# Moving one weight load up in SyncE's program order, at the boundary from the gate blocks to the first output projection

## The reference

```python
z = einsum("btd,dc->btc", rms_norm(x, mix_pre_g), w_in)
u, v, b_gate, c_gate, x_in, r_a, r_b = split(z)
u = gelu(u); v = layer_norm(gelu(v), ...)
y_a = einsum("btc,cd->btd", u * chunk_spatial_mix(v, w_s, b_s), w_a_out)
y_b = einsum("btc,cd->btd", b_gate * short_conv(c_gate * x_in, conv_w), w_b_out)
h = sigmoid(r_a) * y_a + sigmoid(r_b) * y_b
x = x + rms_norm(einsum("btd,de->bte", h, w_o), mix_post_g)
x = x + rms_norm(swiglu(rms_norm(x, ffn_pre_g), w_gate, w_up, w_down), ffn_post_g)
```

## Time and profile before

| what | value |
|---|---|
| time, median of 3 runs | 1629.03 us (1628.82 to 1631.62) |
| time of the profiled execution | 1628.98 us |
| span of the profiled execution | 1627.2 us |
| PE busy | 1608.6 us, 99% of the span |
| DVE / ACT / POOL busy | 64% / 33% / 42% of the span |
| DMA moved | 175.93 MB, mean 108 GB/s |
| mean granted clock of PE | 0.995 of full |

### The profile page before, as it was taken

How to read it: one execution, slowest core, us unless ns; L and a number is a source line. 1 busy time by engine, 2 the same in 40 slices (tenths; PEclk the granted TensorE clock), 3 DMA queues, 4 the chain that set the end, 5 groups by cost and what they waited for, 6 DMA issues and landing times.

```text
span 1627.2 us, 30359 instructions
## 1 busy us (share of the span) xinstructions
PE 1608.6 (99%) x12502; PEld 1554.3 (96%) x12502; DVE 1048.1 (64%) x1588; ACT 541.1 (33%) x816; POOL 679.6 (42%) x486
## 2 busy tenths in 40 slices
PE   8999999999999999899999999999999999999998
PEld 5889999999999999899978899999999999999998
DVE  7867867587583336865438875766666666575766
ACT  4222322222223335332232543222222233452544
POOL 1012444444444443642430216544444443455475
PEclk9999999999999999999999999999999999999999
DMA  5202011321313334353323412533333345572723
GB/s 211 80 0 79 27 53 34 98 79 34 98 60 106 106 106 140 111 177 105 103 100 106 141 47 78 156 105 105 105 105 105 106 126 166 185 234 79 235 104 132
DMA packets 145742, 175.93 MB, mean 108 GB/s; under 512 B 6909, under 2 KB 129397, under 8 KB 145605
## 3 DMA queue, kind: packets, MB, share of 16 engines
q1 hardware_dynamic: 145444, 173.96, 33.2%
q10 hardware_dynamic: 160, 0.04, 0.0%
HBM read 129.52 MB, written 44.49 MB: 107 GB/s over the span
## 4 chain that ended last, share of the span: by engine, by line
PE 93%; DVE 4%; DMA 1%; issue 1%; ACT 1%; POOL 0%; SPq 0%; DVEq 0%; POOLq 0%
PE ps L397 90%; PE ps L471 1%; DMA stage<-in_w_a_out 1%; DMA gv<-in_w_in 0%; DVE tp_f L1946 0%; PE ps L407 0%; PE ps L607 0%; DVE wv_lo_t L1608 0%; DVE small L1594 0%; DVE small L1593 0%; DVE small L1595 0%; DVE tp L1953 0%; PE ps L689 0%; DVE res L2086 0%; DVE q L2083 0%
## 5 line engine op out<-in xcount | busy, mean ns | idle before, releaser
L397 PE MATMUL ps<-tp,ring_hi 128*128 128x258 f32 x7340 | 1192.4, 284 | 6.6 <-POOL ring_lo L1012 6.3
L397 PEld LDWEIGHTS ps<-tp,ring_hi 128*128 128x128 f32 x7340 | 1018.9, 190 | 7.1 <-issue 6.8
L397 PE MATMUL ps<-tp,ring_lo 128*128 128x258 f32 x3670 | 750.4, 283 | 0.0
L397 PEld LDWEIGHTS ps<-tp,ring_lo 128*128 128x128 f32 x3670 | 575.9, 191 | 0.0
L1012 POOL TENSOR_TENSOR ring_lo<-stage,ring_hi 128x512 fp32r<-128x512 f32 (+1 forms) x202 | 311.2, 1550 | 452.2 <-ACT ring_hi L1147 451.9
L1012 POOL TENSOR_TENSOR ring_lo<-ring_f,ring_hi 128x512 fp32r<-128x512 f32 (+1 forms) x216 | 304.6, 1431 | 341.1 <-DVE ring_f L1702 195.7
L1147 ACT ACTIVATE ring_hi<-ring_f 128x512 fp32r<-128x512 f32 (+1 forms) x216 | 135.1, 627 | 481.0 <-DVE ring_f L1697 187.2
L1147 ACT ACTIVATE ring_hi<-stage 128x512 fp32r<-128x512 f32 (+1 forms) x202 | 123.2, 617 | 153.0 <-PE ps L397 85.4
L1694 DVE TENSOR_TENSOR ring_f<-stage 128x512 f32<-128x512 f32 (+1 forms) x54 | 42.2, 782 | 166.9 <-PE ps L397 88.6
L397 PE MATMUL ps<-wv_hi_t,tp 128*128 128x512 f32 x256 | 72.3, 398 | 0.2 <-DVE tp L1616 0.2
L1715 DVE TENSOR_TENSOR s_a<-ps,s_a 128x516 f32<-128x516 f32 (+1 forms) x55 | 37.7, 686 | 52.9 <-PE ps L397 52.4
(11 more groups left out here) (232 smaller groups left out, 1390.2 us busy)
## 6 DMA issues: line engine op xcount, KB each, us to landing
stage<-in_w_in SPq DMA_DIRECT2D x24, 1024.0 KB, 6.1
ht_dram<-ht SPq DMA_DIRECT2D x44, 258.0 KB, 4.8
hid_dram<-hq SPq DMA_DIRECT2D x40, 258.0 KB, 3.0
stage<-in_w_gate SPq DMA_DIRECT2D x10, 1024.0 KB, 6.8
stage<-in_w_up SPq DMA_DIRECT2D x10, 1024.0 KB, 5.4
tp_f<-hid_dram SPq DMA_DIRECT2D x16, 516.0 KB, 6.2
tp_f<-ht_dram SPq DMA_DIRECT2D x16, 516.0 KB, 8.7
stage<-in_w_down SPq DMA_DIRECT2D x8, 1024.0 KB, 8.2
```

Source lines behind the costliest of these rows:

```text
L397: ins = pe.matmul(o, w, xc, start=first and n == 0, stop=last and n == 2)
```

## The change

In SyncE's program, the load of block 25's weights (b = 23, so `load(25)`, into `stage[1]`) used to stand after all four stores of block 23 and after the gate row loads. It now stands right behind the first of the four stores. Nothing is added or removed, and no other engine's program changes.

```diff
                         gate_load(B_A, (0,))
                     sp.wait_ge(gate_ready, 4 * (b - B_RA) + i + 1)
                     sp.dma_start(spill[b % MP, :, n], q[:, n]).then_inc(q_saved[n], 16)
+                    if b == B_A - 1 and i == 0:
+                        load(b + 2)
                 if b == B_A - 1:
                     gate_load(B_A, (2, 1, 3))
-                load(b + 2)
+                else:
+                    load(b + 2)
 
             for b in range(B_A, B_F):
```

## The result

| kernel | median | runs | lowest to highest |
|---|---|---|---|
| before | 1629.36 us | 4 | 1628.82 to 1631.62 |
| changed | 1620.04 us | 4 | 1619.87 to 1620.74 |

The ratio is 0.9941, 95% interval 0.9924 to 0.9958: 9.3 us less. The forecast was 1620.3 us. The profiled execution of the changed kernel took 1619.87 us with a span of 1618.2 us, 9.0 us less than before's.

The account below looks back on a forecast made before the run. PE was held by block 25's late weight load, through DVE and POOL. Idle 6.27 + slow clock 2.37 + product 0's start 0.1 = 8.7 us, off 1628.98: 1620.3 us, range 1618.0 to 1624.0.

Parts of the forecast that it names:

- Place and chain: PE before block 25's product 1: 6.3 us wait traced through POOL's tile 1 and DVE's work to the weight load.
- theory 1: Block 25's weights: their late landing stops PE, us for us beyond a certain cover.
- The load's own wait and landing: SyncE's moved load: no stop at `w_lo`, issued about 622.9, landing in 5.4 us at about 628.3, at worst 634.4.
- The new schedule of DVE and POOL: Block 25: sum 0 and its chain 9.8 us earlier, no other wait ending later; DVE-POOL order effect taken as 0.
- The cover: Block 25's tiles ready ahead of PE's need: 3.5 us at product 1, 2.6 us at product 3.
- The sum: Whole kernel: idle 6.27, slow clock 2.37 and product 0's start 0.1 add to 8.7 us saved.
- the clock's 2.37 us: Product 1 of block 25: 24 matmuls take 5.26 us after the stop, 2.89 at full clock; 2.37 us gained.
- product 0's: Start of block 25's product 0: held some 0.1 us by the rest of tile 0, gained by the change.
- the scatter: Whole-kernel times before: run-to-run width of 2.8 us, 1628.82 to 1631.62, used in setting the forecast's own 1618 to 1623.
- Block 26's load: SyncE's queue: leaves at 642.17 or slightly earlier, lands sooner, not wanted before block 25 has begun; worth 0.

Follow-up runs that it names:

- late_26: Kernel before, block 26's load put behind the first gate row load of block 25, block 25's load unmoved: 1628.93 us, ratio 0.9997.
- sum1_early: Kernel before, DVE's sum 1 of block 25 moved up directly behind sum 0, load order unchanged: 1630.06 us, ratio 1.0008.
- swap_loads: Kernel before, loads of blocks 25 and 26 exchanged so that block 26's goes first: 1632.32 us, ratio 1.0017.
- after_store4: Changed kernel, block 25's load behind the fourth store instead of the first: 1623.09 us, ratio 0.9960 to before.
- after_row1: Kernel before, block 25's load moved up by two gate row loads, still behind the fourth store's landing: 1624.80 us, ratio 0.9975.
- fill: Kernel before, 42 extra transposes on TensorE between products 0 and 1 of block 25: 1629.84 us, ratio 1.0002; repeated, 1629.02 us, 0.9998.
- after_store1_ahead: Changed kernel, block 25's load ahead of the first store of block 23: 1620.01 us, ratio 0.9943 to before.
- fill_half: Kernel before, 21 extra transposes on TensorE between products 0 and 1 of block 25: 1629.78 us, ratio 1.0005.

## Why the prediction was right

- **Place and chain.** Right in each step: the wait of 6.3 us was block 25's weights through sum 0, DVE's run of work, sum 1 and the rest of tile 1. `late_26`, `sum1_early` and `swap_loads` leave no other cause among those tried, and where only the place of the load was changed, landings from 622 to 656 us put the times in the order that theory 1 gives.
- **The load's own wait and landing.** SyncE did not stop at `w_lo`. The landing took 6.2 us where I took 5.4; inside the bounds, and 12 us ahead of need. (Block 24's load, my source for the 5.4, had not quite had the queue to itself: a store had left 0.37 us ahead of it.)
- **The new schedule of DVE and POOL.** Sum 1 at 652.07 (forecast 652.2), rest of tile 1 out at 654.50 (654.6), `a_plain(1)` at 648.63 (648.7). The order of DVE and POOL did change: ACT rounds tile 0 before DVE is through with sum 0, so POOL starts at 641.31, ahead of `at_rest(0)` at 641.63, which now takes 3.40 us, and POOL's two rests take 4.89 us in place of 5.68. Before, `at_rest(0)` was first, by 0.03 us, took 2.30 us, and POOL's rest 3.43. `at_total(2)` got its loss back, 2.85 us in place of 3.97, so the net is 0, as taken. The rule of the Trainium skill weighed in the prediction (SBUF — State Buffer, "Who interferes with whom"), that the one that starts first keeps the port for its whole instruction, agrees with both orders.
- **The cover.** 3.5 and 2.6 us forecast for products 1 and 3; the changed kernel's trace gives 657.71 - 654.50 = 3.2 and 663.49 - 661.2 = 2.3 us, and `after_store4` and `after_row1`, landing 2.3 and 3.4 us beyond the second of these, put the last product 2.4 and 3.4 us later.
- **The sum.** 8.7 us forecast; 9.17 at product 2, 9.0 in the span. The term that was too small is product 0's: it starts at 654.81, not 655.07, and its 24 matmuls had been stretched (3.18 us to 658.25, now 2.90).
- **Wrong: the clock's 2.37 us as a term of its own.** The `fill` runs show that with the stop still there, product 3's tile holds all but 1.4 us of it back. The sum came out because the change moves that tile's chain by the same 9.8 us. Counted from the cover, before's own loss closes the same way: the landing, taken as sum 0's start, is 650.95 - 643.2 = 7.75 us beyond it, and with the 1.4 us that the clock costs at product 3 this is 9.1 us, against 9.07 at the last product. Taken as the gain of filling the stop with other matmuls, the term would have misled.
- **Missed: the scatter.** I counted the 2.8 us between runs as noise of the measurement. The runs point to this wait's own variable length for much of it.
- **Block 26's load.** Right, and worth 0 as taken: it landed after 8.4 us, against 10.9, and PE did not wait for it in either kernel.

## What to carry to other kernels

When a wait's chain ends in a transfer, look at what stands ahead of its issue in the issuing engine's program rather than at its bandwidth alone: here a load that had been allowed since 615.3 us was held until 642.2 by waits for other work, and both places tried ahead of 623 us gave the full gain. Work out the cover from the consumer's order down to the last item, product by product, since a second tile (here product 3's) can stand close behind the first and limit what a partial repair brings. And a kernel whose runs scatter more than its neighbours may be telling of a transfer's variable landing on its critical chain.

## What was not expected of the hardware

- The time from the fourth 258 KB store's issue to the issue of the gate row load that waits for it was 2.3 to 4.5 us in executions that were alike up to there, but for a shift of up to 0.9 us from their start.
- A 1 MB load of these blocks took 5.2 to 6.7 us to land with one 258 KB transfer right ahead of it, 6.8 us with block 24's 1 MB issued 2.0 us ahead (`after_store1_ahead`), and 7.5 to 9.0 us behind three 258 KB transfers, a second 1 MB following or not.
- PE's granted clock was 1.00 behind stops of 1.27, 2.39 and 2.57 us in `after_store4`, `after_row1` and `fill_half`. It had fallen behind the stops of 3.80 and 3.41 us in `sum1_early` (0.58 over 658.6 to 661 and over 672.4 to 674), of 5.0 and 4.8 us in `swap_loads` (0.54 over 659.8 to 662, 0.50 over 669.2 to 671) and of 6.27 us before.
- One `instruction` packet of 0.02 MB among the last stores went with 0.8 to 1.4 us more between the last product and the end of the span, in three of three kernels.
